# VectorE's side work in a fused decoder step: normalised chunks rebuilt during the key tiles, logits and maxima handled one piece a page, the state update set in front of a chunk's low part

## The reference

```
layer 0: proj = x @ w_in;  q, k, v, o, gates        (8 heads, key width 64, value width 128)
         mLSTM in chunks:  h = num / max(|den|, exp(-m))
         C_new = ae * C + sum_s ws * k_s v_s^T       per sequence and head (the matrix memory)
         x = LN(ALPHA * x + (sigmoid(o) * h) @ w_out)
         x = LN(ALPHA * x + sq_relu(x @ w_up) @ w_down)
layer 1: k, v = x @ w_kv (new rows, also outputs);  q = x @ w_q
         samples: scores of q with all past keys, 8 pages of 128 keys per sequence from a paged pool;
                  of the 4 blocks of 256 keys the one with the lowest q . mean(k) is left out;
                  logits + ALiBi, softmax over the chosen blocks and the own keys, times the values
         prompt:  causal attention inside its one block
         x = LN(ALPHA * x + attention @ w_out);  x = LN(ALPHA * x + MLP(x))
```

## Time and profile before

| | |
|---|---|
| median of 3 runs | 906.5 us (906.05 to 908.79) |
| the profiled execution: its own time / its span | 906.84 us / 905.1 us |
| PE busy | 889.7 us (98% of the span) |
| DVE, ACT, POOL busy | 624.3, 440.1, 65.7 us |
| mean granted TensorE clock | 0.994 of full speed |
| key stage, first page turned to last page scored | 421.7 to about 547 us of the span |
| output product of layer 0, as far as the change touches it | about 132 to 168 us |

### The profile page before, as it was taken

How to read it: one execution, slowest core, us unless ns; L and a number is a source line. 1 busy time by engine, 2 the same in 40 slices (tenths; PEclk the granted TensorE clock), 3 DMA queues, 4 the chain that set the end, 5 groups by cost and what they waited for, 6 DMA issues and landing times.

```text
span 905.1 us, 18714 instructions
## 1 busy us (share of the span) xinstructions
PE 889.7 (98%) x7472; PEld 841.0 (93%) x7472; DVE 624.3 (69%) x1090; ACT 440.1 (49%) x826; POOL 65.7 (7%) x83
## 2 busy tenths in 40 slices
PE   9999999999999999999999999999999999999996
PEld 8999997999999999999888788988999999999985
DVE  6477667888976475677575847447668797757536
ACT  5445766376345363445344363345537634526421
POOL 0010007400000000330000000000230000000000
PEclk9999999999999999999999999999999999999998
DMA  9982215664455444466988998999945545554301
GB/s 291 260 254 94 94 50 138 187 198 141 141 176 149 140 140 154 166 231 215 333 302 290 348 360 313 400 408 355 291 140 160 167 146 183 154 169 141 140 1 59
DMA packets 132331, 182.78 MB, mean 202 GB/s; under 512 B 5875, under 2 KB 113211, under 8 KB 132244
## 3 DMA queue, kind: packets, MB, share of 16 engines
q1 hardware_dynamic: 126938, 177.56, 59.4%
q0 software_dynamic: 640, 2.10, 0.9%
q10 hardware_dynamic: 4666, 1.92, 0.9%
HBM read 175.24 MB, written 6.32 MB: 201 GB/s over the span
## 4 chain that ended last, share of the span: by engine, by line
PE 89%; DVE 5%; ACT 2%; issue 1%; POOL 1%; DMA 1%; SPq 0%; ACTq 0%; DVEq 0%; POOLq 0%
PE ps L639 23%; PE ps L641 23%; PE ps L640 23%; PE ps L1041 5%; PE ps L1083 3%; PE ps L1141 3%; DVE k_turned L2066 1%; PE ps L929 1%; PE ps L931 1%; PE ps L930 1%; DMA raw<-in_w_in_a_dram 1%; PE ps L653 1%; PE ps L756 0%; PE ps L940 0%; PE ps L938 0%
## 5 line engine op out<-in xcount | busy, mean ns | idle before, releaser
L1665 DVE TENSOR_TENSOR w_lo<-raw,w_hi 128x1024 fp32r<-128x1024 f32 x192 | 238.1, 1243 | 108.8 <-ACT w_hi L1258 108.7
L1258 ACT ACTIVATE w_hi<-raw 128x1024 fp32r<-128x1024 f32 x192 | 202.3, 1056 | 225.4 <-PE ps L641 201.2
L639 PE MATMUL ps<-x_hi,w_hi 128*128 128x322 f32 (+1 forms) x888 | 279.2, 314 | 0.0
L641 PE MATMUL ps<-x_hi,w_lo 128*128 128x322 f32 (+1 forms) x888 | 276.2, 311 | 0.0
L640 PE MATMUL ps<-x_lo,w_hi 128*128 128x322 f32 (+1 forms) x888 | 275.8, 311 | 0.0
L639 PE MATMUL ps<-h_hi,w_hi 128*128 128x320 f32 x552 | 171.4, 311 | 0.0
L640 PE MATMUL ps<-h_lo,w_hi 128*128 128x320 f32 x552 | 171.0, 310 | 0.0
L641 PE MATMUL ps<-h_hi,w_lo 128*128 128x320 f32 x552 | 171.0, 310 | 0.0
L639 PEld LDWEIGHTS ps<-x_hi,w_hi 128*128 128x128 f32 x888 | 168.0, 189 | 1.6 <-issue 1.0
L640 PEld LDWEIGHTS ps<-x_lo,w_hi 128*128 128x128 f32 x888 | 168.5, 190 | 0.2
L641 PEld LDWEIGHTS ps<-x_hi,w_lo 128*128 128x128 f32 x888 | 167.4, 189 | 0.0
(11 more groups left out here) (349 smaller groups left out, 980.2 us busy)
## 6 DMA issues: line engine op xcount, KB each, us to landing
raw<-in_w_up_dram SPq DMA_DIRECT2D x32, 1024.0 KB, 5.7
raw<-in_w_down_dram SPq DMA_DIRECT2D x32, 1024.0 KB, 5.2
page<-in_cache_k_dram SPq DMA_DIRECT2D x64, 512.0 KB, 5.5
page<-in_cache_v_dram SPq DMA_DIRECT2D x64, 512.0 KB, 9.8
raw<-in_w_in_a_dram SPq DMA_DIRECT2D x11, 1024.0 KB, 9.3
raw<-in_w_kv_dram SPq DMA_DIRECT2D x8, 1024.0 KB, 5.3
raw<-in_w_out_a_dram SPq DMA_DIRECT2D x4, 1024.0 KB, 5.2
raw<-in_w_q_b_dram SPq DMA_DIRECT2D x4, 1024.0 KB, 5.2
```

The costliest lines, as they stand in the source:

```text
L639: mm(out, WH[PLACE[t]][:, k, :], hi[:, k, 0:width], start=(k == 0), stop=False)
L641: last = mm(out, WL[PLACE[t]][:, k, :], hi[:, k, 0:width], start=False, stop=(k == 7))
L1258: A(WH[PLACE[t]][:, :, :], raw_tile(t), ACT.Copy)\
L1665: V.tensor_tensor(WL[PLACE[t]][:, :, :], raw_tile(t), WH[PLACE[t]][:, :, :].bitcast(F32), ALU.subtract)\
```

## The change

Three things are written in another place, and one is cut in two. In the output product of layer 0, `state(n + 1)` stands in front of `x_low(0, n)`. In the key stage `rebuilt(1, n)` for n = 0 to 6 moves from behind the copies of pages 10 to 22 into `k_extra`, in front of the weight split and `kvq`; for n = 7 it goes behind page 47. At the last key tile `kvq` goes in front of the weight split. `logits(0, 3)` moves from page 35 to page 36, `block_max(0)` is cut into one reduction of four blocks behind page 38 and one behind page 39, and `biases(0)` moves from page 41 to page 43.

```diff
@@ the output product of layer 0 (DVE)
                 if n < 7:
                     split_to(t + 3)
+                if n < 7:
+                    state(n + 1)
                 x_low(0, n)
                 split_to(t + 3)
-                if n < 7:
-                    state(n + 1)
@@ k_extra (DVE)
                 if p == K_FIRST + 16:
                     own_read(p)
+                elif not odd and n == 7:
+                    kvq(8 + n)
+                    split_to(8 * Q_WK + n + 2)
                 elif not odd:
+                    rebuilt(1, n)
                     split_to(8 * Q_WK + n + 2)
                     kvq(8 + n)
@@ block_max (DVE)
-            def block_max(G):
+            def block_max(G, halves=(0, 1)):
                 _, mxb, _, omx, _, _, _ = parts(G)
                 dve.wait_ge(s_Lr, 4 * G + 4)
-                V.tensor_reduce(mxb, L[G][:, :, :].rearrange("p a (n k) -> p (a n) k", n=4), AX.X, ALU.max)
-                own(V.tensor_reduce(omx, PO[:, G, :, :], AX.X, ALU.max))
+                for a_ in halves:
+                    V.tensor_reduce(mxb[:, 4 * a_:4 * a_ + 4], L[G][:, a_, :].rearrange("p (n k) -> p n k", n=4),
+                                    AX.X, ALU.max)
+                if 1 in halves:
+                    own(V.tensor_reduce(omx, PO[:, G, :, :], AX.X, ALU.max))
@@ the loop over pages P (DVE)
                 elif P == 35:
                     logits(0, 1)
+                elif P == 36:
                     logits(0, 3)
+                elif P == 38:
+                    block_max(0, (0,))
                 elif P == 39:
-                    block_max(0)
+                    block_max(0, (1,))
                 elif P == 41:
                     left_out(0)
+                elif P == 43:
                     biases(0)
+                elif P == 47:
+                    rebuilt(1, 7)
                 if P % 2 and K_FIRST <= p <= K_FIRST + 16:
                     k_extra(p)
-                if P % 2 == 0 and 5 <= p < 13:
-                    rebuilt(1, p - 5)
```

## The result

The changed kernel takes 901.69 us, the median of 5 runs (900.86 to 902.97), against 906.5 before (905.83 to 908.79): a ratio of 0.9943, with a 95% interval of 0.9931 to 0.9954. That is 4.8 us faster; 901.2 was forecast. So I compare stretches, not points of time.

A forecast was written before the change was run, and what follows sets the result against it. PE, busy 98% of the span, was taken as the bound. Gains 2.6 + 0.3 + 2.4 = 5.3 off the 906.5 median gave 901.2 us; own range 899.8 to 902.4, wider range 899.6 to 903.8.

The forecast's parts named there:

- Key tiles: Key stage, tiles 1 to 6: rebuilt chunks fit VectorE's idle stretches, four long periods become clean, 2.6 us gained.
- up to 0.3 of lateness costs nothing: Key stage: VectorE's first pair of copies ends at 434.8, PE wants that bank at 435.1.
- Last key tile: From the last key tile on: first wait grows 0.45, second falls from 1.2 to 0.5; gain 0.3, bounds -0.5 and 1.2.
- State update: Output product of layer 0: C runs inside VectorE's wait for ScalarE; 2.4 us gained, bounds 1.8 and 3.3.
- The cap by VectorE's chain: Output product of layer 0: PE could gain 3.29, but VectorE's last `x_low` limits it to 2.4.
- from nothing to 0.46, I take 0.1: Output product of layer 0: GpSimd begins sooner with `state(1)` in front of `x_low(0, 0)`, so the wait-ending `x_hi` comes 0.1 earlier.
- 2.07 without its overlap: Output product of layer 0: VectorE reaches its last `x_low` earlier by the C block done inside its wait, 2.07.
- The clock: Output product of layer 0, behind PE's wait for C: the stretch at clock 0.59, costing 1.52, goes with the wait.
- rival B: The clock still falls once, at the new wait or in its old place; price 1.5, 902.7 us; chance 0.17.
- Transfers: SP's weight load waits for the last key tile's split, 1.5 later, with pages behind it: no cost, bounds 0 and 1.5.
- The rival, a page late behind that load: Behind the last key tile: the tail gets worse and page 42 comes late; 903.5 us; chance 0.08.
- A: The forecast itself, whole kernel: 901.2 us, own range 899.8 to 902.4; chance 0.64.

The follow-up runs named there:

- chunks alone: Kernel before with only the rebuilt chunks moved into key tiles 1 to 6 and the last behind page 47: 904.18 us, ratio 0.9955 to 0.998.
- tail alone: Kernel before with only the part from the last key tile on (`kvq`, logits, maxima, `biases`) changed: 906.54 us, ratio 0.9987 to 1.0004.

## Why the prediction was right, point by point

- **Key tiles, 2.6.** Right in mechanism and size (2.64 alone). In the profiled execution 0.89 went again, to a late store. Its cushion, "up to 0.3 of lateness costs nothing", is 0.1 to 0.2, and it hangs on the bank of the key tile, not on that of the first copies.
- **Last key tile, 0.3.** Measured 0.17. Its two terms, 0.45 more on the first wait and 0.7 less on the second, came as forecast (0.45, 0.73); 0.11 was lost between them.
- **State update, 2.4.** Faster, and the C block as forecast, but this is the step that was mis-sized: 3.27, at its upper bound of 3.3. The cap by VectorE's chain was the right thing to ask for; two of its terms were wrong. For "from nothing to 0.46, I take 0.1", GpSimd's start, 1.74 was measured: I priced only when it starts, not that by starting ahead of a weight split it takes half as long. For "2.07 without its overlap", C, 1.39. So the wait of 0.9 for `x_lo` did not come. The sentence that drew on the Trainium skill there looked only at `x_low` against GpSimd; the split was the one that mattered. In after the addition starts 0.2 behind the start of that `x_low` and still takes only 1.47.
- **The clock.** It went with the wait, as expected: in none of the ten profiles without the wait for C does the granted clock fall there. But the wait does not always bring the fall: of the three profiles that have it (before, chunks alone, tail alone), two show half clock behind it and the third does not. And the 1.52 that PE lost to it was worth 0.1 in the old order, since VectorE's chain was the bound. What a fall would cost in the new order, rival B's price, no profile shows.
- **Transfers.** "No cost" held for after. The rival, a page late behind that load, begins with the split only a few instructions later than where the change put it (2.07 for page 44).
- **The sum.** 5.3 forecast, 6.0 by the stretches, 5.2 and 6.2 by the ratios of the two sets of runs; the first interval, 4.2 to 6.3, holds both sums. That the median lay so near the forecast is partly luck: the state's term was 0.9 short, and what hid it in the median (late stores and the start, as in the profiles, or noise) is not shown. A's own range, 899.8 to 902.4, does not quite follow from the bounds of its terms, which add up to 3.9 to 7.1: 899.4 to 902.6.

## What to carry to other kernels

Before pricing a move by an engine's own list, look at what the moved instructions start on another engine, and beside what that engine then runs: here about half of what the state update gained came from GpSimd's addition starting ahead of a weight split and no longer waiting for it. A filler that fits an idle stretch with 0.3 to spare is paid back whenever the engine that ends the stretch is late (0.89 and 0.46 in two profiles); moving that engine's work forward too may help, though no profile here caught a late store with it. And when an instruction is moved later, read what stands behind its semaphore in the transfer queue: a split moved behind a few copies left the DMA engines empty for 4.5 us.

## What the runs showed of the hardware

- A weight split on VectorE takes 1.21 to 1.23 alone, or where GpSimd waits for it, and 1.50 to 1.93 where it lies behind or among GpSimd's instructions; GpSimd's 128x512 addition takes 1.47 where it starts 0.64 ahead of a split, and 2.62 to 3.01 where the two start within 0.22 of each other.
- Issuing a 32 KB store on ScalarE mostly takes 0.50, but in four of the profiles one or more took 1.0 to 1.6. What delays it is open.
- The granted clock fell to half (1.2 GHz) behind one and the same wait of PE, 0.78 by its row, in the profiles of two kernels and not in that of a third whose work up to there is the same.
